# Four shared weight buffers of a two-block transformer kernel begin at other places within a 256-byte period

## What is computed

```python
proj = x @ w_in[l]                                   # 1024 x 3592
mix = jnp.concatenate([o_a, o_r], axis=-1).astype(dtype) @ w_o[l]
h = _causal_depthwise_conv(x @ w_up[l], conv_w[l], conv_b[l])     # 1024 x 5632
ffn = (jax.nn.gelu(a, approximate=False) * u) @ w_down[l]         # 2816 x 1024
...
q, k, v, hv, hx1, hx2, gna, ghy = jnp.split(h @ w_in[i], IN_SPLITS, axis=-1)
x = x + g1 * gated_merge(gna, ghy, y_na, y_hy, w_na_o[i], w_hy_o[i], w_out[i])
x = x + g2 * swiglu(h2, ffn_w1[i], ffn_w3[i], ffn_w2[i])
```

## Time and profile before

| | before |
|---|---|
| median of three runs | 1568.44 us |
| the profiled execution, its own time | 1566.09 us |
| its span, first to last instruction | 1564.3 us |
| PE busy | 1515.6 us, 97% |
| LDWEIGHTS (PEld) busy | 1300.6 us, 83% |
| DVE busy | 1022.0 us, 65% |
| ACT busy | 691.9 us, 44% |
| mean granted TensorE clock | 0.992 |

### The profile page before, as it was taken

How to read it: one execution, slowest core, us unless ns; L and a number is a source line. 1 busy time by engine, 2 the same in 40 slices (tenths; PEclk the granted TensorE clock), 3 DMA queues, 4 the chain that set the end, 5 groups by cost and what they waited for, 6 DMA issues and landing times. The chain is left out here.

```text
span 1564.3 us, 21018 instructions
## 1 busy us (share of the span) xinstructions
PE 1515.6 (97%) x8432; PEld 1300.6 (83%) x8432; DVE 1022.0 (65%) x1547; ACT 691.9 (44%) x1020; POOL 435.9 (28%) x367
## 2 busy tenths in 40 slices
PE   5999998999999999999999999998999999999997
PEld 5778886788888888888988888886788999999886
DVE  7676457769677866678643643338855799985334
ACT  5644346755533354233523344443445544543322
POOL 0024315621511211000260032214342666660002
PEclk9999999999999999999999999999999999999999
DMA  8342112363244523665424332314462123224211
GB/s 310 109 148 92 64 55 95 133 221 118 108 163 161 178 91 121 244 252 204 133 108 148 108 98 91 118 49 161 142 234 87 53 109 109 107 108 162 85 78 54
DMA packets 50987, 203.61 MB, mean 130 GB/s; under 512 B 18528, under 2 KB 18784, under 8 KB 32138
## 3 DMA queue, kind: packets, MB, share of 16 engines
q1 hardware_dynamic: 37346, 172.04, 30.7%
q0 software_dynamic: 8576, 28.29, 5.1%
q10 hardware_dynamic: 4968, 1.94, 0.5%
HBM read 181.24 MB, written 21.00 MB: 129 GB/s over the span
## 5 line engine op out<-in xcount | busy, mean ns | idle before, releaser
L583 PE MATMUL ps<-xl,whi 128*128 128x512 f32 (+1 forms) x1136 | 393.1, 346 | 0.0
L1853 DVE TENSOR_TENSOR wlo<-raw,whi 128x2048 fp32r<-128x2048 f32 x89 | 221.8, 2493 | 142.7 <-ACT whi L1212 142.5
L1212 ACT ACTIVATE whi<-raw 128x512 fp32r<-128x512 f32 (+1 forms) x191 | 232.4, 1223 | 127.6 <-PE ps L584 84.3
L582 PE MATMUL ps<-xh,whi 128*128 128x256 f32 (+1 forms) x768 | 262.4, 342 | 6.2 <-DVE xl L1897 6.2
L584 PE MATMUL ps<-xh,wlo 128*128 128x256 f32 (+1 forms) x768 | 256.8, 334 | 0.0
L583 PEld LDWEIGHTS ps<-xl,whi 128*128 128x128 f32 x1136 | 216.2, 190 | 24.2
L582 PEld LDWEIGHTS ps<-xh,whi 128*128 128x128 f32 x768 | 146.8, 191 | 28.3 <-issue 15.6
L584 PEld LDWEIGHTS ps<-xh,wlo 128*128 128x128 f32 x768 | 146.7, 191 | 14.8
L582 PE MATMUL ps<-xhr,whi 128*128 128x512 f32 (+1 forms) x368 | 136.8, 372 | 0.7 <-DVE xl L1897 0.7
L584 PE MATMUL ps<-xhr,wlo 128*128 128x512 f32 (+1 forms) x368 | 136.4, 371 | 0.0
L2611 DVE TENSOR_TENSOR wlo<-raw,whi 128x512 fp32r<-128x512 f32 x98 | 89.7, 948 | 0.2 <-ACT whi L1212 0.2
(11 more groups left out here) (468 smaller groups left out, 3663.9 us busy)
## 6 DMA issues: line engine op xcount, KB each, us to landing
raw<-in_w_in SPq DMA_DIRECT2D x35, 1024.0 KB, 5.0
raw<-in_ffn_w SPq DMA_DIRECT2D x33, 1024.0 KB, 4.8
raw<-in_ada SPq DMA_DIRECT2D x24, 1024.0 KB, 4.8
raw<-in_w_up SPq DMA_DIRECT2D x22, 1024.0 KB, 4.8
raw<-in_w_down SPq DMA_DIRECT2D x11, 1024.0 KB, 5.3
xd<-X POOLq DMA_DIRECT2D x8, 512.0 KB, 6.9
td<-vr POOLq DMA_DIRECT2D x16, 256.0 KB, 3.6
raw<-td SPq DMA_DIRECT2D x4, 1024.0 KB, 4.8
```

Of the source, the lines that this page charges most:

```text
L582: pe.e.matmul(o, lh, rh, start=start, stop=False)
L583: pe.e.matmul(o, lh, rl, start=False, stop=False)
L1212: m = ac.e.activation(dst, src, func, **more)
L1853: up(ve.e.tensor_tensor(lo, raw[conv_at[j] % 3][:, :], hi.bitcast(F32), ALU.subtract), "wlo")
```

## The change

The four shared buffers become 8 elements (32 bytes) longer each, and the kernel works in a slice of each that begins 16 or 0 bytes behind its start. With the 32 bytes that each adds for the next, the slices begin at +16 (`whi` 0), +48 (`whi` 1), +64 (`wlo` 0) and +112 (`wlo` 1). A filler of 128 bytes behind them makes up the 256, so that all that is allocated later lies 256 bytes further on and is at +0 again.

```diff
         X, Xr = twins("X", [P, 4, D], ctx)
         raw = [sb("raw", [P, 2048]) for _ in range(3)]
-        whi = [sb("whi", [P, 2048], F32R) for _ in range(2)]
-        wlo = [sb("wlo", [P, 2048], F32R) for _ in range(2)]
+
+        whi = [sb("whi", [P, 2056], F32R)[:, 4:2052] for _ in range(2)]
+        wlo = [sb("wlo", [P, 2056], F32R)[:, 4 * i:4 * i + 2048] for i in range(2)]
+        sb("fill", [P, 32])
         bc, bc_r = twins("bc", [P, 2 * D], ctx)
```

## The result

The changed kernel takes 1582.47 us (median of four runs, 1581.29 to 1586.39), the kernel before beside it 1568.68 us. The ratio is 1.0094, with a 95% interval of 1.0069 to 1.0119: 13.8 us slower. No change was forecast.

The account below looks back on a forecast made before the run. PE was taken as the bound: number of products times distance between starts. Products 0, DVE 0, ACT 0, DMA 0 left the median of 1568.4, so 1568 us was predicted, range 1560 to 1585.

Parts of the forecast that it names:

- What bounds the kernel: Whole kernel: PE busy 1515.6 of 1564.3 us, so time is the number of products times the distance between their starts.
- The zeros for DVE and ACT: DVE's subtractions and ACT's `whi` writes: 0 us from shifted places; at most 68 ns more per 512 elements on DVE.
- I take 0 for this term: Distance between starts of PE's products: shifted places change it by 0 us.
- The price is the same ... whether the shared buffer is loaded, streamed, or neither: PE's products: mean 389 to 390 ns in all three cases, taken as support for a fixed price and 0 change.
- Moves the point where they meet and not how often they meet: PE's load and stream do not keep step, so a start 16 to 112 bytes off should change nothing.
- The rows of L1024: Key windows, plain float32 at +0, +32, +96, +128: 0.70 us each per four matmuls, so offsets cost and gain nothing there.
- The term that was called the largest: Extra 13.2 ns on each of 6576 products reading a shared buffer: 87 us, 5.5% of the time.
- Both readings of the prediction: The 13 ns per product: load and stream meeting in memory, removable by places, or a fixed price of changing stationary operand.
- The meeting is real: Rival: PE's load and stream meet and new places take it away; faster, 1513, about 1540 or some 1485; chance 0.15.
- Wider reading units: slower: Rival: TensorE reads wider units, starts inside one cost 6.7 ns; 1579 streamed alone, 1605 with loads; chance 0.18.
- some 1485: Time forecast if all 87 us of the extra price on PE's products went, less the DVE bound.
- scatter: Measurement scatter around no change (0.64): said to take 0.03 to either side; 0.02 added to faster and to slower.

Follow-up runs that it names:

- map4: Products alone, reference's work left out: 512 columns, order of three, four places, two lead-ins, fixed or moving addresses; loaded at +16 took 226.7 ns, then 233.3 ns.
- all64: All four shared buffers at +64, against the kernel before the change: 13.7 us slower.
- all32: All four shared buffers at +32, against the kernel before the change: 1587.78 us beside 1566.87, ratio 1.0133.
- hi_only: `whi` at +16 and +48, both `wlo` at +0, against the kernel before the change: 13.5 us slower.
- lo_only: `wlo` at +64 and +112, both `whi` at +0, against the kernel before the change: 19.3 us slower.
- fast64: Only the fast stage's quarters (256 columns) moved to +64, whole pieces at +0, against the kernel before the change: 1562.33 us beside 1566.27, ratio 0.9972.
- map3: Products alone, reference's work left out: order of three, loaded, streamed or both at +0 to +240; 512 columns at +0 took 226.7 ns, both at +16 230.0 ns.

## Why the prediction was wrong

**What bounds the kernel: right.** PE's distances, not waits, in the main. The zeros for DVE and ACT held as prices of places (682 to 684 ns against a bound of 68 ns more). What the sum had no term for is that a shift in time changes which instructions meet: the longer wait for `xl` near 394 us and the lower clock behind it, 4.9 us in the profiled execution.

**"I take 0 for this term": wrong, and it is the step that failed.** It measured +13.5 us (+16.2 for 512 columns, -2.7 for 256). Of the reasons for it:
- "The price is the same ... whether the shared buffer is loaded, streamed, or neither": true, and no evidence. All of those operands were at +0. Distances in whole multiples of 256 bytes are one and the same place, as `map4` shows; the rows had a single point of the curve and I read it as a flat curve.
- "Moves the point where they meet and not how often they meet": by this a start elsewhere could change nothing, and that was false. The same pair of places is steady at 226.7 or at 233.3 ns (`map4`), and other places range from 226.7 to 236.7. That loads and streams keep step, in rhythms, is how these steady distances are read here; the reads themselves are in no trace. The Trainium skill, "TensorE: Matmul & The Clock Gate", Part 2, step 1, has the two ports independent, so that loading takes nothing from the running matmul; here a load that starts 32 bytes off lengthens the distance from 226.7 to 233.3 ns, and the measurement decides.
- The rows of L1024, where +32 and +96 cost nothing: right in their numbers. They are plain float32, which takes two cycles a column; nothing of the kind follows for float32r, and the prediction said this without drawing the consequence.

**The term that was called the largest** was 13 ns for each product. None of the maps got a 512-column product under 226.7 ns, so for those it is a fixed price at the best place. For 256 columns 6.7 of the 13.3 ns go away at +64. Both readings of the prediction were partly right, each for another width.

**The rivals.** "The meeting is real": real, but with the sign turned round. I took equal places for the worst case; for 512 columns they are the best, and that is why the wide products could gain nothing there. "Wider reading units: slower" named the side and gave 1579 for streamed operands alone, near the 1582.5 that was measured, by a wrong mechanism: it let +64 go free (`all64` costs 13.7 us) and let +32 cost no more than +16 (`all32` 20.9 against 13.1). What may be true of it is 3.3 ns at odd multiples of 16 bytes with both operands there. By the Trainium skill, "SBUF — State Buffer", Door 1, note on cachelines, lines are 16 bytes, and a start at a multiple of 16 crosses no more of them; that 3.3 ns is not in it. That the time fell inside the stated range is luck: its upper part was there for this rival's price.

**Its sums.** Two were off, without a part in the failure: 1568 less 87 us with 9.8 given back to DVE's bound is 1491 and not "some 1485", and scatter is said to take 0.03 to either side where 0.02 is added to each.

**What the profile would show** was named in the right place: groups with a shared buffer against those without (393 against 389 ns), and distances of 512 and 256 columns.

**Open.** What in the memory or in TensorE makes the rhythms, and what chooses one, is not shown: the runs show distances only. Between the sums of distances and the measured times 1 to 4.5 us remain (`hi_only` and `lo_only` most). The traces show the wait near 394 us and the lower clock behind it for them, but one execution of each run is traced, and no run kept that wait apart from the places.

## What to carry to other kernels

When a loop is bound by TensorE at full rate, where operands begin within a 256-byte period is worth a look, for float32r at least: wrong places cost this kernel up to 1.3% (`all32`), and better ones than +0 gave 0.3% (`fast64`). Keep both operands at the same place (a multiple of 32 bytes) for 512 streamed columns, and for 256 try the loaded one at +64 against the streamed one. Measure it in the kernel, since a map of products alone does not always say which rhythm the kernel falls into. And a trace in which a quantity never varies says nothing about what happens when it does: before a term is called zero from rows, ask whether any row has the new value.

## What the hardware showed that was not expected

- The most common steady distances are steps: 226.7, 230.0, 233.3 and 236.7 ns are 544, 552, 560 and 568 cycles of 2.4 GHz, that is 32 to 56 more than the 512 columns; 120.0 and 113.3 ns are 288 and 272, or 32 and 16 more than 256. In `fast64` the groups of three in the fast stage take 3 x 117.8 ns = 848 cycles, the steps of 16 again, now for the group.
- Two steady rates for the same instructions and addresses, 226.7 and 233.3 ns, by what ran before them.
- Equal places are best for 512 columns, while with 256 columns no place of the loaded operand in `map3` was slower than +0: 120.0 ns against 113.3 at +64.
- The halves of the change cost 13.5 and 19.3 us, the whole 13.8 (in distances alone 9.1, 14.9 and 13.5).
- The same subtraction of DVE's took 0.69 us when it started 0.05 us ahead of a product of POOL's, and 2.90 us when it started 0.05 us behind it.
- A wait that grew from 0.74 to 3.06 us was followed by 5.9 us at the lower clock level: 27 products at 213 ns instead of 120, 2.6 us more for the clock alone.
